# A two-layer recurrent decoder trunk on one core: where the modulation matmuls and the RWKV steps stand, and how the layer norm is shared out

## The reference

```python
mods = (jax.nn.silu(c) @ ada_w + ada_b).reshape(B, 3, 3, 1, D_MODEL)
def modulate(t, i):
    return t * (1.0 + mods[:, i, 1]) + mods[:, i, 0]
def residual(t, i, out, w):
    return _layer_norm(ALPHA * t + w * (1.0 + mods[:, i, 2]) * out, ln_g[i], ln_b[i])

x = residual(x, 0, _swiglu(modulate(x, 0), ffn_wg[0], ffn_wu[0], ffn_wd[0]), 0.5)
proj = modulate(x, 1) @ w_in
p_rw, p_gla, p_ml = _split(proj, [RW_PROJ, GLA_PROJ, ML_PROJ])
...
mix = jnp.concatenate([o_rw, o_gla, o_ml], axis=-1) @ w_out
x = residual(x, 1, mix, 1.0)
x = residual(x, 2, _swiglu(modulate(x, 2), ffn_wg[1], ffn_wu[1], ffn_wd[1]), 0.5)
```

## Time and profile before

| What | us |
|---|---|
| Median of the timed runs | 1681.7 |
| Timed runs, lowest to highest | 1667.69 to 1681.84 (3 runs) |
| Profiled execution, its own time | 1677.3 |
| Span of its trace, first to last instruction | 1675.5 |
| TensorE busy in the span | 1608.5 |
| VectorE busy | 936.3 |
| ScalarE busy | 667.0 |
| GpSimd busy | 203.6 |

### The profile page before, as it was taken

The page is one execution under the profiler, slowest core; times in us unless marked ns, Lnnn a source line. Parts: engine busy times, 40 slices in busy tenths (PEclk is TensorE's granted clock), DMA queues, the critical chain, the costliest instruction groups (busy, mean ns, idle before and its releaser), DMA issues. The chain is left out here.

```text
span 1675.5 us, 32875 instructions
## 1 busy us (share of the span) xinstructions
PE 1608.5 (96%) x14052; PEld 1480.5 (88%) x14052; DVE 936.3 (56%) x1605; ACT 667.0 (40%) x985; POOL 203.6 (12%) x271
## 2 busy tenths in 40 slices
PE   5999999999999999999999999999999999999997
PEld 2999998998767789999989999989877768899996
DVE  1544545586653775555474544466946456655544
ACT  2333334563323355333364333355532334543333
POOL 1000011100222330000110000210022242100011
PEclk9999999999997799999999999999989669999998
DMA  8765555533443174444755545654412116444441
GB/s 310 279 225 209 171 204 204 176 116 100 139 146 104 62 261 143 148 150 151 254 212 198 192 145 173 233 173 138 124 35 84 54 39 244 148 148 148 151 152 68
DMA packets 103864, 268.57 MB, mean 160 GB/s; under 512 B 39560, under 2 KB 42024, under 8 KB 103464
## 3 DMA queue, kind: packets, MB, share of 16 engines
q1 hardware_dynamic: 99304, 263.86, 46.3%
q10 hardware_dynamic: 4416, 2.62, 0.6%
HBM read 260.19 MB, written 6.26 MB: 159 GB/s over the span
## 5 line engine op out<-in xcount | busy, mean ns | idle before, releaser
L2410 DVE TENSOR_TENSOR wlo<-raw,whi 128x1024 fp32r<-128x1024 f32 x300 | 367.6, 1229 | 323.2 <-ACT whi L2261 320.9
L2261 ACT ACTIVATE whi<-raw 128x1024 fp32r<-128x1024 f32 x300 | 316.2, 1055 | 295.3 <-PE psV L2073 262.2
L2071 PE MATMUL psA<-XH,whi 128*128 128x320 f32 x1104 | 345.0, 313 | 7.9 <-DVE wlo L2410 7.5
L2073 PE MATMUL psA<-XH,wlo 128*128 128x320 f32 x1104 | 342.7, 310 | 0.0
L2072 PE MATMUL psA<-XL,whi 128*128 128x320 f32 x1104 | 342.6, 310 | 0.0
L2071 PE MATMUL psV<-XH,whi 128*128 128x320 f32 x848 | 267.1, 315 | 0.2
L2072 PE MATMUL psV<-XL,whi 128*128 128x320 f32 x848 | 263.8, 311 | 0.0
L2073 PE MATMUL psV<-XH,wlo 128*128 128x320 f32 x848 | 263.7, 311 | 0.0
L2071 PEld LDWEIGHTS psA<-XH,whi 128*128 128x128 f32 x1104 | 208.8, 189 | 10.8 <-issue 9.5
L2072 PEld LDWEIGHTS psA<-XL,whi 128*128 128x128 f32 x1104 | 208.7, 189 | 0.3
L2073 PEld LDWEIGHTS psA<-XH,wlo 128*128 128x128 f32 x1104 | 208.7, 189 | 0.0
(11 more groups left out here) (413 smaller groups left out, 2012.1 us busy)
## 6 DMA issues: line engine op xcount, KB each, us to landing
raw<-weights_dram SPq DMA_DIRECT2D x400, 512.0 KB, 3.4
own<-weights_dram SPq DMA_DIRECT2D x56, 512.0 KB, 5.9
in_xh<-weights_dram SPq DMA_DIRECT2D x6, 512.0 KB, 4.2
in_xl<-weights_dram SPq DMA_DIRECT2D x6, 512.0 KB, 5.0
raw<-weights_dram SPq DMA_DIRECT2D x6, 384.0 KB, 3.6
raw<-weights_dram SPq DMA_DIRECT2D x8, 256.0 KB, 3.8
in_hl<-weights_dram SPq DMA_DIRECT2D x4, 512.0 KB, 5.4
ZS<-st_rw_dram SPq DMA_DIRECT2D x2, 768.0 KB, 4.4
```

Source lines behind the costliest of these rows:

```text
L2071: mm(out, split_hi(n)[:, k], hi[:, kt], start=first, stop=False)
L2073: return mm(out, split_lo(n)[:, k], hi[:, kt], start=False, stop=last)
L2261: activation(split_hi(n), buffer(DENSE[n]), ACT.Copy).then_inc(hi_done, 1)
L2410: tt(split_lo(n), buffer(DENSE[n]), split_hi(n).bitcast(F32), ALU.subtract).then_inc(lo_done, 1)
```

## The change

It does five things. The order of projections, RWKV and convolution steps is written out (`PROJ_MIXED`). Every gap gets at most two groups: the third group of the first gap goes to layer 1's mixers (8 groups now), that of layer 1's last gap to the up product of layer 2 (4 groups), that of layer 2's first gap and the two of layer 2's out gap to layer 2's mixers (6 groups), so that the latter gap holds none. `LATE` becomes one list for each layer; in layer 2 five of the groups are late, where two were. Folds in a gap all follow behind the first four tiles. In the norm ScalarE instead of VectorE squares and copies the mean, from the bank, signalled by `mean_full`, `mean_squared` and `mean_kept`. The table for logarithm and exponential is loaded at the start of `product` on ScalarE instead of at the norm, and VectorE's split of a weight chunk goes ahead of its first norm instruction.

```diff
--- before.py
+++ after.py
@@ -88,18 +88,19 @@
 
 LEVELS = (6, 6, 3)
 
-RW_PRE = (2, 2, 2, 2, 3, 3, 2, 2, 2)
-RW_TWICE = (3, 5, 7)
-CV_AT = (4, 9, 12, 15, 18)
+PROJ_MIXED = ("rw 23 24 rw 25 26 rw cv 11 12 rw 13 rv 14 cv 15 rw 16 17 cv 27 rw 28 rv 19 cv 20 rw 21 cv 22 rw 29 rv 30 rw").split()
 
 RW_INVERSE = 9 + 2 * (max(LEVELS) - 1)
 
 GL_FIRST, ML_FIRST = 3, 4
 
 
-LATE = ("rw ml ada gl rw ml ada gl ml ada_ rw gl ml ada rw gl ml ada ada_ gl ada rw ml ada_ gl ada rw ml ada gl ada_ ml ada rw fold "
-        "gl rw ml su mix rs rw rs su hi.0 rs lo.0 rw hi.1 rw hi.2 lo.1 early.0 rw lo.2 early.1 rw").split()
-IN_LATE = (3, 2)
+LATE = (
+    ("rw ml ada gl rw ml ada gl ml ada rw gl ml ada rw gl ml ada ada gl ada rw ml ada gl ada rw ml ada gl ada ml ada rw fold "
+     "gl rw ml su mix rs rw rs su hi.0 rs lo.0 rw hi.1 rw hi.2 lo.1 early.0 rw lo.2 early.1 rw").split(),
+    ("rw ada ml ada gl ada rw ml ada gl ml ada rw gl ada ml ada rw gl ada ml ada gl ada ada rw ada ml ada gl ada ada rw ml ada ada "
+     "gl ada ml ada ada rw fold gl rw ml su mix rs rw rs su hi.0 rs lo.0 rw hi.1 rw hi.2 lo.1 early.0 rw lo.2 early.1 rw").split())
+IN_LATE = (3, 5)
 
 EARLY_FIRST = 5
 
@@ -167,7 +168,7 @@
 
     bursts = [[("ada", *group, q) for q in range(4)] + [("fold", *g) for g in groups[max(n - 1, 0):n]]
               for n, group in enumerate(groups)]
-    return bursts + [[("fold", *groups[-1])]]
+    return bursts + [[("fold", *group)] for group in groups[-1:]]
 
 
 def gap_groups(groups):
@@ -194,25 +195,19 @@
     out = after([step for steps in tiles for step in steps], folds)
     steps, left = product(("down", L, 0), 0, in_gaps[0])
     out += steps
-    rest = [("proj", L, t) for t in PROJ_ORDER[NRW:]]
-    for k in CV_AT:
-        rest.insert(k, ("cv", L))
     out += after([("proj", L, t) for t in PROJ_ORDER[:NRW]], left)
-    out += spread([slot for k, w in enumerate(RW_PRE)
-                   for slot in ([(("rw", L), 1), (("rv", L), w - 1)] if k in RW_TWICE else [(("rw", L), w)])], rest)
+    out += [("proj", L, int(name)) if name.isdigit() else (name, L) for name in PROJ_MIXED]
     rw, gl, ml = [("rw", L)], [("gl", L)], [("ml", L)]
     first = ml + gl + [("cv", L)] + (ml + gl) * (GL_FIRST - 1) + ml * (ML_FIRST - GL_FIRST)
     together = spread([(rw[0], int(k > 1)) for k in range(RW_INVERSE)], first)
     out += spread([(step, 1) for step in together], ada_groups(in_tail[:-IN_LATE[L]]))
     chunks = ada_groups(in_tail[-IN_LATE[L]:])
-    for name in LATE:
-        if name == "fold" or name == "ada_" and IN_LATE[L] < 3:
-            continue
-        if name not in ("ada", "ada_"):
+    for name in LATE[L]:
+        if name not in ("ada", "fold"):
             out.append((name.split(".")[0], L, *map(int, name.split(".")[1:])))
             continue
         out.append(chunks.pop(0))
-        while chunks and chunks[0][0] == "fold":
+        while len(chunks) > 1 and chunks[0][0] == "fold":
             out.append(chunks.pop(0))
     assert not chunks
     steps, left = product(("out", L), 1, in_gaps[1])
@@ -227,11 +222,10 @@
 
     out = ada_groups(groups(0, 0, 0, 1, 2, 3)) + [("enter", 0)]
     steps, left = layer_plan(0, groups(0, 0, 4, 5) + groups(0, 1, 0, 1, 2, 3),
-                             (groups(0, 1, 4, 5) + groups(0, 2, 0), groups(1, 0, 2, 3), groups(1, 0, 4, 5) + groups(1, 1, 0)),
-                             groups(0, 2, 1, 2, 3, 4, 5) + groups(1, 0, 0, 1))
+                             (groups(0, 1, 4, 5), groups(1, 0, 2, 3), groups(1, 0, 4, 5)),
+                             groups(0, 2, 0, 1, 2, 3, 4, 5) + groups(1, 0, 0, 1))
     out += steps
-    steps, left = layer_plan(1, groups(1, 1, 1, 2, 3), (groups(1, 1, 4, 5) + groups(1, 2, 0), groups(1, 2, 4, 5), []),
-                             groups(1, 2, 1, 2, 3), left)
+    steps, left = layer_plan(1, groups(1, 1, 0, 1, 2, 3), (groups(1, 1, 4, 5), [], []), groups(1, 2, 0, 1, 2, 3, 4, 5), left)
     return out + steps
 
 
@@ -660,7 +654,7 @@
 
         half_bank, proj_bank = {}, {}
 
-        var_bank = {}
+        var_bank, mean_bank = {}, {}
         low_bank = {}
 
         def at(name, v):
@@ -2176,10 +2170,11 @@
                     for x in (ZSUM, QSUM):
                         bank = bV.open()
                         mm(bank[:, 0:TOK], con("mean1024", P), x[:], start=True, stop=False)
-                        bV.close()
+                        bV.close(freed=None if means else (sem("mean_kept"), s + 1))
                         means.append(bank)
+                    mean_bank[s] = means[0]
                     pe.wait_ge(sem("z_ready"), (s + 1) * DT)
-                    mm(means[0][:, 0:TOK], con("mean1024", P), ZT[:, DT - 1], start=False, stop=True).then_inc(sem("bankV_full"), 1)
+                    mm(means[0][:, 0:TOK], con("mean1024", P), ZT[:, DT - 1], start=False, stop=True).then_inc(sem("mean_full"), 1)
                     pe.wait_ge(sem("sq_ready"), (s + 1) * DT)
                     mm(means[1][:, 0:TOK], con("mean1024", P), SQ[:, DT - 1], start=False, stop=True).then_inc(sem("bankV_full"), 1)
 
@@ -2292,6 +2287,7 @@
                         result(after, DT - 1)
 
                 def product(n0, kts, s):
+                    nc.scalar.preload_act_table_set("natural_log_exp_and_others")
                     for d in range(DT):
                         if d == DT - 1 and s % 3 == 1:
 
@@ -2301,11 +2297,13 @@
                         A.do(activation(SQ[:, d], ZT[:, d], ACT.Square), sem("sq_ready"))
 
                 def norm(s):
-                    nc.scalar.preload_act_table_set("natural_log_exp_and_others")
+                    act.wait_ge(sem("mean_full"), s + 1)
+                    A.do(activation(VR[:], mean_bank[s][:, 0:TOK], ACT.Square), sem("mean_squared"))
+                    A.do(activation(MN[:], mean_bank[s][:, 0:TOK], ACT.Copy), sem("mean_kept"))
+                    act.wait_ge(sem("var_ready"), s + 1)
+                    rsqrt(A, VR[:], sem("sd_ready"))
                     if s in THREE:
                         rows(*THREE[s])
-                    act.wait_ge(sem("var_ready"), s + 1)
-                    rsqrt(A, VR[:], sem("sd_ready"))
                     modulate(s + 1 if s < 3 * DEPTH - 1 else None, s)
                     if s % 3 != 0 and s < 3 * DEPTH - 1:
                         nc.scalar.preload_act_table(ACT.Silu)
@@ -2482,18 +2480,15 @@
                     split_to(m + LOCK - 1)
 
                 def norm(s):
+                    split_to(n_next + LOCK - 1)
+                    fV.skip()
                     bank = fV.take()
-                    V.do(nc.vector.tensor_copy(MN[:], bank[:, 0:TOK]), sem("bankV_free"))
-                    V.settle()
-                    V.do(tt(VR[:], MN[:], MN[:], ALU.mult))
-                    V.settle()
-                    bank = fV.take()
+                    vec.wait_ge(sem("mean_squared"), s + 1)
                     V.do(tt(VR[:], bank[:, 0:TOK], VR[:], ALU.subtract), sem("bankV_free"))
                     V.settle()
                     V.do(ts(VR[:], VR[:], 0.0, LN_EPS / ALPHA ** 2, ALU.max, ALU.add), sem("var_ready"))
+                    vec.wait_ge(sem("mean_kept"), s + 1)
                     V.do(tt(ZT[:, 0], ZT[:, 0], MN[:], ALU.subtract))
-
-                    split_to(n_next + LOCK - 1)
                     vec.wait_ge(sem("sd_ready"), s + 1)
                     V.settle()
                     modulate(s + 1 if s < 3 * DEPTH - 1 else None, s)
```

## The result

The changed kernel takes 1666.6 us (median of 20 runs, 1657.5 to 1678.8), the kernel before, on the same occasions, 1677.9 us (20 runs, 1664.8 to 1685.2). The ratio is 0.9943, with a 95% interval from 0.992 to 0.9965: 0.57% faster. Forecast were 1671.9 us and a gain of 7.6 us; it is about 9.6 us by the ratio, and 11.3 between the two medians. The profiled execution took 1668.7 us with a span of 1666.6, against 1677.3 and 1675.5.

The account below looks back on a forecast made before the run. TensorE, busy 96%, bounds the kernel. Norm and gaps -8.9, projections -5.8, up product +2.4, layer 1's mixers +2.3, layer 2's +2.4 sum to -7.6 us: 1671.9 us, midway between 1669.7 and 1674.1; range 1658 to 1687.

Parts of the forecast that it names:

- The projections: Both layers' projections: new order removes TensorE's 3.0 us wait for a low half of weights; gain 2.9 us per layer, 5.8 in all.
- projections give nothing: Rival: in the projections the wait only moves behind the last one; -1.8 us in all, 1677.7 us; chance 0.2.
- The norm chain: Norms: ScalarE takes over the mean; VectorE gets on 1.26 us earlier in gap 1, last norm 0.5 earlier.
- The load priced at nothing: ScalarE's table load at the product's start: assumed hidden, costing 0; uncovered, up to 1.28 us per product, 7.7 in all.
- What ended a three-group gap: Norm gaps with three modulation groups: the groups took longer than the norm's chain, by 1.03 us in the first gap.
- gaps 1, 3 and 4: Norm gaps after down products: fewer groups and a shorter chain gain about 1.6, 1.8 and 2.2 us.
- Gap 5: Layer 2's out gap, now empty: TensorE starts earlier with an equally long slow stretch; gain 2.5 us, bounds 0.1 and 4.9.
- the second gap: Norm gap after layer 1's out product: same two groups, split pieces set the end; gain 0.25 us.
- The clock: Layer 2's mixers: extra filler chunks take 6 us of slow-clock time back, bounds 0 and 15.3.
- rival of the clock: Two, on layer 2's mixers: clock stays up, 1662.6 us, chance 0.2; or chunks land in slow stretches, 1685.3, chance 0.15.
- the slower side: Rival: chunks land in slow stretches of layer 2's mixers, costing over 10 us extra there; +5.8 us, 1685.3; chance 0.15.

Follow-up runs that it names:

- order_only: Kernel before with only the written order of projections, RWKV and convolution steps changed; ratio 0.9941, mean 1666.7 us.
- load_back: Changed kernel with the table load put back to the start of the norm; one run, 1683.5 us.
- norm_only: Kernel before with only the norm's part (ScalarE squares and copies the mean, table load and split moved ahead); ratio 0.9978, mean 1673.5 us.
- split_back: Norm's part and written order, groups in old gaps, VectorE's split back behind its first norm instructions; first tile at 9.96 us in gap 1, no total given.
- norm_order: Kernel before with the norm's part and the written order, groups in their old places; ratio 0.9935, mean 1666.9 us.
- only_l2: Changed kernel with only layer 2's groups moved; gaps 1 and 3 and the up product hold three groups; ratio 0.9938, mean 1668.8 us.
- keep_l2: Changed kernel with layer 2's gaps, late list and mixers as before; ratio 0.990, side by side again 0.9936, mean of both occasions 1664.8 us.
- gap5_kept: Changed kernel with two groups put back into layer 2's out gap, its mixers then holding four groups; ratio 0.9899, mean 1663.1 us.
- groups_only: Kernel before with only the modulation groups moved, order and norm as before; ratio 0.9999, mean 1676.6 us.
- norm_undone: Changed kernel with the norm as it was before; ratio 0.9971, mean 1673.0 us.

## Why the prediction was right, and where it was not

**The projections: right in mechanism, undersized.** The walk through VectorE's queue held. It said that VectorE would idle for the sixth step's root (4.6 us said, 2.96 measured behind a later split), that the last split would be just in time, and that the loss would move behind the last projection. The term that was too large was that tail: from the last projection's end to the first transposes 1.4 + 1.8 = 3.2 us said, 2.4 measured (405.92 to 408.34), because VectorE does its three bonus instructions (done at 408.23) while the matmuls that feed them still run (to 407.70), so that TensorE waits for 0.64 only. So 4.0 and 3.8 us came, not 2.9 each. Two readings in that sum were wrong and nearly cancel: the slow matmuls behind the old stall are some 13, worth 1.5 us (their starts are 0.27 us apart, not 0.15, from 400.6 to 403.8), not 19 and 2.3; and the ninth step's matmuls, taken off with 0.8, take 1.4 (404.28 to 405.65). That they cancel is luck. The rival "projections give nothing" is refuted by order_only.

**The norm chain: right.** 1.17 us measured for 1.26 in gap 1, 0.5 for 0.5 at the end. The load priced at nothing cost nothing to be seen: in layer 1's out product the first split starts 1.86 us after the last mixer activation's start (576.76 to 578.62), before it was 1.87. And load_back shows that its old place would have cost 0.8 us per gap. The Trainium skill (ScalarE: Activation LUTs, What ACT_TABLE_LOAD costs) states a drain of about 1.38 us with each load. None is to be seen here: in load_back 0.02 us lie between the instruction before and the load, and 0.01 between the load and the next.

**What ended a three-group gap: wrong in the reason.** The prediction let the filler's length end the old gap. Of the 1.03 us by which it found the first gap too long, 0.85 (9.32 less the 8.47 of norm_only) were the last chunk's wait for its transfer, held by the buffer of the weights that VectorE split too late. split_back shows it. Without that wait the filler is about as long as the old chain (8.47 against a first piece ready at 8.29). The gain that the prediction gave to gaps 1, 3 and 4 (1.6, 1.8, 2.2) was nearly reached: TensorE is through with the first four tiles 1.4, 1.6 and 2.1 us earlier after the norm. But 0.8, 0.9 and 1.5 of it come in norm_only already, so the larger half belongs to the norm's part, and the groups get little: with the split ahead, a third group delays the first tile by 8.47 - 7.27 = 1.2 us, and TensorE regains half of that, because it waits for piece 8 in the shorter gap. The stage from norm 3 to norm 4 is the clean reading, since in these profiles its clock never falls: 244.9 in norm_only, norm_order and only_l2; 246.7 in the whole change, keep_l2 and gap5_kept. Moving the group out of that gap into the up product costs 1.8 us in each. In the product a group takes 2.34 (four chunks and a fold, 911.16 to 913.50 in TensorE's timeline), as forecast; so the gap got back 0.5 to 0.6.

**Gap 5: right in place, wrong in worth.** The first tile was to come at 7.9 us, and came at 7.84. But 2.5 us of gain were counted from one execution in which transfers were late. The stage after it takes 241.6 us in that profile, but 237.8 to 239.2 with the same two groups in the gap in order_only, norm_only, norm_order and keep_l2, and 238.0 with none. Emptying the gap is worth 1 us at most. The clock works against more: TensorE idles for 5.3 to 5.6 us in the empty gap, and in all six profiles with that gap empty 2.9 to 4.4 us of what follows run at 1.2 GHz; with two groups in the gap three of eight profiles have no stretch at the low clock up to norm 6. The prediction counted the slow stretch on both sides, from the one profile that it had. The same holds for the second gap, whose first tile came at 8.96 with a slow stretch behind it in the profile of the whole change, at 8.65 in its second one, at 9.01 in load_back, and at 7.84 to 8.41 in all others, with the same instructions there in three of them (gap5_kept and keep_l2 twice): transfers are the limit there (DMA share 0.97 from 606 to 616 us), and +1.3 us in the table is that, not the change. Layer 1's mixers are the same kind of reading: 200.0 us in this profile of the whole change, 196.9 in the other, where less of them ran at the low clock.

**The clock: right in direction, not located.** 6 us were to come back from layer 2's mixers. groups_only gives 6 over the kernel, at a price of 4.8. Which moved groups bring it is not shown: keep_l2, which leaves layer 2's groups, and only_l2, which moves only them, both have 133 us at the low clock. The groups' net can't be told from nil (ratio 0.9999); together with the other parts they make the kernel slower by 7.2 us at an equal clock (whole change against norm_order) and take 18 us off the low clock, worth 5.6. The whole change's mean is 1.5 us above norm_order's, less than can be told apart. Neither rival of the clock came: layer 2's stretch at the low clock stayed (27 us), and the moved groups cost less than the 10 us from which the slower side would have decided. The price is 7.2 on top of the norm's and order's parts and 4.8 alone. The norm's part doesn't explain this: on top of the order alone, with the old norm, the groups cost 7.8 (norm_undone against order_only, 1670.5 and 1662.7). With standard errors of 0.9 to 1.1 an interaction with the order is possible; no run separates it.

That the sum (-7.6) came near -9.6 is in part luck: the errors had opposite signs. The projections gave 7.8, not 5.8; the fifth gap 1 at most, not 2.5. And of the 9.6 only 3.4 stand at an equal clock, while 6 go with less time at the low clock over the whole kernel.

## What to carry to other kernels

Before filler is blamed for the length of a gap, compare its own time with the gap: if it is shorter, look for what its last piece waits for, and which instruction frees that buffer; here moving this instruction cost nothing. Where an engine does weight preparation and other work in one order, walk its queue with measured durations, put every preparation ahead of the long steps, and let the loss fall where nothing queues behind. And where executions scatter by more than the effect, read the deterministic stages in the profile, and compare totals at an equal clock beside the plain ones.

## What the runs showed of the hardware

TensorE's clock is down at 1.2 GHz in stretches where it is busy without a break: 23.71 of 24 us in layer 1's mixers, before and after, with the same 337 matmuls. Over 189 runs 1 us of it goes with 0.31 us of time. Half a microsecond would be expected if every matmul there took twice as long; why it is less, no run shows. Filler in the mixers went with less time at the low clock (146 to 127 us in groups_only, 145 to 127 from norm_order to the whole change), but the groups' places alone don't tell which part of it does. In the norm gaps the clock was down for 3.4 us after TensorE had idled for 1.9 us (gaps 1 and 3 of norm_undone and groups_only, not gap 4), and never after 1.1 us (gaps 1, 3 and 4 of the changed kernel). Which stretch will fall in a given execution stays open: keep_l2 and the whole change have the same matmuls in layer 1's mixers, and their executions differ by whole stretches there and in layer 2.
